# The last expert's down product: column halves of w_down one after the other, with scatter, squares and products between them

## The reference

```python
def expert_choice_swiglu(h, w_router, w_gate, w_up, w_down):
    cap = EC_CAPACITY_FACTOR * seq // N_EXPERTS          # 64
    aff = softmax(h @ w_router)
    g, idx = top_k(swapaxes(aff, 1, 2), cap)             # each expert its 64 tokens
    xin = h[idx]
    a, u = xin @ w_gate, xin @ w_up                      # 64 x 1024 x 1024 each, per expert
    y = (silu(a) * u) @ w_down * g[..., None]
    return zeros.at[idx].add(y)                          # scattered back to the tokens
...
x = x + expert_choice_swiglu(rms_norm(x, norm2_g), ...)
return rms_norm(x, normf_g)
```

## Time and profile before

| | us |
|---|---|
| median of 3 runs | 883.68 (882.5 to 883.97) |
| span of the profiled execution (first to last instruction) | 882.2 |
| the profiled execution's own time around the span | not given apart |
| TensorE busy in the span | 853.8 (97%) |
| VectorE, ScalarE, GpSimd busy | 358.2, 268.3, 26.9 |
| last matmul of the last down ends | 869.41 |
| first output transfer issued | 874.81 |

### The profile page before, as it was taken

The page is one execution under the profiler, slowest core; times in us unless marked ns, Lnnn a source line. Parts: engine busy times, 40 slices in busy tenths (PEclk is TensorE's granted clock), DMA queues, the critical chain, the costliest instruction groups (busy, mean ns, idle before and its releaser), DMA issues.

```text
span 882.2 us, 10559 instructions
## 1 busy us (share of the span) xinstructions
PE 853.8 (97%) x4287; PEld 522.3 (59%) x4287; DVE 358.2 (41%) x638; ACT 268.3 (30%) x469; POOL 26.9 (3%) x47
## 2 busy tenths in 40 slices
PE   9999999999999999999999999999998988988996
PEld 8898876687878888889534443343433433334332
DVE  5378877576606344327322313132221311311413
ACT  6233766685624233227101010010100101001213
POOL 1050000000000000002000000000000000000001
PEclk9999999999999999999999999999999999999999
DMA  9730212023134335843999999999999999999993
GB/s 287 166 96 1 72 48 96 1 68 89 42 120 115 107 86 145 316 204 144 387 408 417 422 429 429 428 428 428 426 427 426 428 427 427 428 429 429 427 418 152
DMA packets 80372, 238.70 MB, mean 271 GB/s; under 512 B 8003, under 2 KB 63427, under 8 KB 65605
## 3 DMA queue, kind: packets, MB, share of 16 engines
q1 hardware_dynamic: 75040, 235.94, 67.9%
q10 hardware_dynamic: 5284, 2.09, 1.0%
HBM read 235.92 MB, written 2.10 MB: 270 GB/s over the span
## 4 chain that ended last, share of the span: by engine, by line
PE 81%; DMA 11%; DVE 3%; ACT 2%; issue 1%; ACTq 0%; POOL 0%; DVEq 0%; POOLq 0%; SPq 0%
PE psum L1521 18%; PE psum L1553 12%; DMA wslot<-in_w_down 11%; PE psum L1054 11%; PE psum L1055 10%; PE psum L1056 10%; PE psum L1478 3%; PE psum L1572 3%; PE psum L1236 2%; PE psum L1248 2%; PE psum L1206 1%; PE psum L1222 1%; PE psum L1533 1%; PE psum L1486 1%; PE psum L1258 1%
## 5 line engine op out<-in xcount | busy, mean ns | idle before, releaser
L1521 PE MATMUL psum<-wslot,xinT 128*64 128x512 f32 x1016 | 226.9, 595 | 5.8 <-DMA wslot<-in_w_gate 2.7
L1521 PEld LDWEIGHTS psum<-wslot,xinT 128*64 128x64 f32 x1016 | 70.3, 137 | 145.6 <-issue 133.9
L1553 PE MATMUL psum<-wslot,actT 128*64 128x512 f32 x504 | 114.1, 597 | 8.7 <-DMA wslot<-in_w_down 8.7
L1054 PE MATMUL psum<-hT_hi,w_hi 128*128 128x512 f32 x208 | 82.8, 398 | 0.0
L1056 PE MATMUL psum<-hT_hi,w_lo 128*128 128x512 f32 x208 | 81.2, 391 | 0.0
L1055 PE MATMUL psum<-hT_lo,w_hi 128*128 128x512 f32 x208 | 81.2, 391 | 0.0
L1553 PEld LDWEIGHTS psum<-wslot,actT 128*64 128x64 f32 x504 | 34.7, 137 | 76.4 <-issue 69.0
L1748 DVE TENSOR_TENSOR w_lo<-w_raw,w_hi 128x1024 fp32r<-128x1024 f32 (+1 forms) x46 | 52.9, 1174 | 52.7 <-ACT w_hi L706 52.6
L993 ACT ACTIVATE actT<-psum 128x512 f32<-128x512 f32 x16 | 9.6, 598 | 185.5 <-PE psum L1533 185.5
L2123 DVE TENSOR_TENSOR x<-x,psum 128x512 f32<-128x512 f32 x56 | 34.7, 682 | 74.7 <-PE psum L1572 74.7
L2115 DVE TENSOR_TENSOR y_lo<-psum,y_hi 64x512 fp32r<-64x512 f32 x32 | 22.0, 689 | 103.1 <-ACT y_hi L1003 102.6
(11 more groups left out here) (268 smaller groups left out, 1303.9 us busy)
## 6 DMA issues: line engine op xcount, KB each, us to landing
wslot<-in_w_gate SPq DMA_DIRECT2D x27, 2048.0 KB, 29.3
wslot<-in_w_up SPq DMA_DIRECT2D x27, 2048.0 KB, 29.9
wslot<-in_w_down SPq DMA_DIRECT2D x24, 2048.0 KB, 28.3
w_raw<-in_w_in SPq DMA_DIRECT2D x34, 512.0 KB, 4.8
wslot<-in_w_down SPq DMA_DIRECT2D x15, 1024.0 KB, 30.5
wslot<-in_w_gate SPq DMA_DIRECT2D x10, 1024.0 KB, 11.3
wslot<-in_w_up SPq DMA_DIRECT2D x9, 1024.0 KB, 10.7
w_raw<-in_w_out SPq DMA_DIRECT2D x8, 512.0 KB, 5.0
```

The costliest lines, as they stand in the source:

```text
L1054: pe.matmul(out_, s_hi, m_hi, start=(k == 0), stop=False)
L1521: mm = pe.matmul(bank[2 * e + n][CAP * f:CAP * f + CAP, :], xinT[:, HALF * h + k, CAP * e:CAP * e + CAP], wslot[place_of(m)][:, k % PART, ...
L1553: mm = pe.matmul(bank[4 + e][CAP * f:CAP * f + CAP, :], actT[:, e, k, CAP * h:CAP * h + CAP], wslot[place_of(m)][:, k % PART, SEQ * f:SEQ ...
```

## The change

The last expert's down runs per column half. Its w_down is loaded in four quarters, each four steps k (one h) by 512 columns, in the order (h, f) = (0,0), (1,0), (0,1), (1,1), into the same four places. `last_down(h, f)` issues the four matmuls of a quarter. y of f = 0 is taken out, scattered, and for tiles 0 and 1 squared and multiplied by the gain, between the quarters; add_rows(2,0) moves in front of the second quarter. Pieces are now scattered and squared with f = 0 first. `GAINED` holds the four pieces of f = 0: VectorE multiplies them by the gain early, and they are scaled later, (3,0) and (2,0) by ScalarE, (0,0) and (1,0) by VectorE in SBUF. Where both ScalarE and VectorE read a piece from PSUM, one waits for the other. GpSimd's three counters become one, and the squares' scrap buffer moves.

```diff
-        LAST_PIECES = [(0, 0), (1, 0), (0, 1), (1, 1), (3, 0), (3, 1), (2, 0), (2, 1)]
-        SQUARED = [(c, f) for c in SUM_TILES for f in range(2)]
-        GAINED = [(1, 1), (3, 0)]
-        FINISHED = [(0, 0), (0, 1), (1, 0), (3, 1), (2, 0), (2, 1)]
-        OUT_PIECES = [(0, 0), (0, 1), (1, 0), (1, 1), (3, 1), (3, 0), (2, 0), (2, 1)]
+        LAST_PIECES = [(c, f) for f in range(2) for c in SUM_TILES]
+        SQUARED = LAST_PIECES
+        GAINED = [(1, 0), (0, 0), (2, 0), (3, 0)]
+        GAINED_FIRST = [(1, 0), (2, 0)]
+        SCALED_ACT = [(3, 0), (2, 0)]
+        FINISHED = [(0, 1), (0, 0), (1, 1), (1, 0), (3, 1), (2, 1)]
+        OUT_PIECES = [(0, 1), (0, 0), (1, 1), (1, 0), (3, 0), (3, 1), (2, 0), (2, 1)]
...
+                if m >= LAST_DOWN:
+                    f, h = divmod(m - LAST_DOWN, 2)
+                    rows = rows_of((LAST_DOWN + 2 * h) // 2).rearrange("p (k n) -> p k n", k=HALF)
+                    sp.dma_start(by_columns(m), rows[:, :, SEQ * f:SEQ * f + SEQ]).then_inc(w_slot_in[place], 16)
+                    return
...
                 for f in range(2):
+                    if last:
+                        wait_part_used(act_, last_part(1, f))
                     act_.activation(y_hi[CAP * e:CAP * e + CAP, SEQ * f:SEQ * f + SEQ],
                                     bank[4 + e][CAP * f:CAP * f + CAP, :], ACT.Copy).then_inc(y_hi_done, 1)
+                    if last and f == 0:
+                        square_sum(0)
+                        square_sum(1)
...
+            def last_down(h, f, between):
+                p, m = PAIRS - 1, last_part(h, f)
+                wait_part_in(pe, m)
+                for k in range(HALF):
+                    mm = pe.matmul(bank[5][CAP * f:CAP * f + CAP, :], actT[:, 1, k, CAP * h:CAP * h + CAP],
+                                   by_columns(m)[:, k, :], start=(h == 0 and k == 0), stop=(h == 1 and k == HALF - 1))
+                    if k == HALF - 1:
+                        mm.then_inc(w_slot_used[place_of(m)], 1)
+                    between(k)
...
+            def behind_first(k):
+                if k == 1:
+                    add_rows(1, 0)
+                if k == 3:
+                    pe.wait_ge(y_lo_done, 4 * (PAIRS - 1) + 2)
+                    add_rows(2, 0)
...
+            last_down(0, 0, behind_first)
+            last_down(1, 0, behind_others)
+            last_down(0, 1, behind_others)
             pe.wait_ge(y_hi_done, 4 * PAIRS - 1)
+            pe.wait_ge(y_lo_done, 4 * PAIRS - 1)
+            give_rows(0, 0)
+            give_rows(1, 0)
+            last_down(1, 1, behind_others)
+            give_rows(3, 0)
+            give_rows(2, 0)
             pe.wait_ge(y_hi_done, 4 * PAIRS)
             pe.wait_ge(y_lo_done, 4 * PAIRS)
+            give_rows(0, 1)
+            give_rows(1, 1)
+            give_rows(3, 1)
             add_rows(2, 1)
+            give_rows(2, 1)
...
+                    if (p, e, f) == (PAIRS - 1, 1, 0):
+                        dve.wait_ge(gf_done, 2)
+                        gain(1, 0)
+                        gain(0, 0)
...
             def finish(c, f):
                 cols = slice(SEQ * f, SEQ * f + SEQ)
                 dve.wait_ge(rstd3, SUM_TILES.index(c) + 1)
+                if (c, f) in GAINED:
+                    dve.wait_ge(gained, GAINED.index((c, f)) + 1)
+                    dve.tensor_scalar(fin[:, c, cols], fin[:, c, cols], rstd[:, c:c + 1], None, ALU.mult)\
+                        .then_inc(fin_done, 1)
+                    return
...
-            gain(1, 1)
+            gain(2, 0)
             gain(3, 0)
```

More of the change, by code:

```diff
@@ L202, in encoder_block @@
     fin = sb("fin", [NT, D], W0)
-    junk = sb("junk", [2, SEQ], 60)
+    junk = sb("junk", [2, SEQ], 105.5)
     g2 = small[:, 8:16]
@@ L245, in encoder_block @@
         sumsq_done = sem("sumsq_done")
-        ms_done = sem("ms_done")
+        pool_step = sem("pool_step")
         rstd_done = sem("rstd_done")
@@ L257, in encoder_block @@
         a_sumsq = sem("a_sumsq")
-        a_ms = sem("a_ms")
         a_rstd = sem("a_rstd")
@@ L287, in encoder_block @@
         sumsq2 = sem("sumsq2")
-        ssq2_summed = sem("ssq2_summed")
         rstd2 = sem("rstd2")
@@ L335, in encoder_block @@
         ssq3 = sem("ssq3")
-        ssq3_summed = sem("ssq3_summed")
         rstd3 = sem("rstd3")
@@ L428, in encoder_block, with last_part, by_columns @@
         tenants = [[m for m in range(N_PARTS) if place_of(m) == i] for i in range(SLOTS + len(ONCE))]
+        LAST_DOWN = N_PARTS - 4
+        def last_part(h, f):
+            return LAST_DOWN + 2 * f + h
+        def by_columns(m):
+            return wslot[place_of(m)].rearrange("p k n -> p (k n)").rearrange("p (k n) -> p k n", k=HALF)
         def turn_of(m):
@@ L613, in _ @@
                 cols = slice(SEQ * f, SEQ * f + SEQ)
-                if (c, f) in GAINED:
-                    sp.wait_ge(fin_act_done, GAINED.index((c, f)) + 1)
+                if (c, f) in SCALED_ACT:
+                    sp.wait_ge(fin_act_done, SCALED_ACT.index((c, f)) + 1)
                 else:
@@ L626, in _, with settle, power, power_of_means @@
             pool.wait_ge(neg_half_set, 1)
-            def power(sums, into, n, width, counted, done, first):
-                pool.tensor_scalar(into, sums, 1.0 / width, EPS, ALU.mult, ALU.add).then_inc(counted, 1)
-                pool.wait_ge(counted, first + 1)
+            steps = [0]
+            def settle(ins):
+                ins.then_inc(pool_step, 1)
+                steps[0] += 1
+                pool.wait_ge(pool_step, steps[0])
+            def power(sums, into, n, width, done):
+                settle(pool.tensor_scalar(into, sums, 1.0 / width, EPS, ALU.mult, ALU.add))
                 pool.tensor_tensor(into, into, neg_half[:, 0:n], ALU.pow).then_inc(done, 1)
-            def power_of_means(c, i):
+            def power_of_means(c):
                 first, second = (ssq_half[:, 2 * c + f:2 * c + f + 1] for f in range(2))
-                pool.wait_ge(ssq3, 2 * i + 2)
-                pool.tensor_scalar(rstd[:, c:c + 1], second, first, EPS, ALU.add, ALU.add).then_inc(ssq3_summed, 1)
-                pool.wait_ge(ssq3_summed, i + 1)
+                pool.wait_ge(ssq3, SQUARED.index((c, 1)) + 1)
+                settle(pool.tensor_scalar(rstd[:, c:c + 1], second, first, EPS, ALU.add, ALU.add))
                 pool.tensor_tensor(rstd[:, c:c + 1], rstd[:, c:c + 1], neg_half[:, 0:1], ALU.pow).then_inc(rstd3, 1)
@@ L643, in rstd_of_x @@
                 pool.wait_ge(sumsq_done, c + 1)
-                power(ssq[:, c:c + 1], rstd[:, c:c + 1], 1, D, ms_done, rstd_done, c)
+                power(ssq[:, c:c + 1], rstd[:, c:c + 1], 1, D, rstd_done)
             for c in range(NT):
@@ L651, in _ @@
                 pool.wait_ge(a_sumsq, c + 1)
-                power(ssqA[:, w * c:w * c + w], rstdA[:, w * c:w * c + w], w, HD, a_ms, a_rstd, c)
+                power(ssqA[:, w * c:w * c + w], rstdA[:, w * c:w * c + w], w, HD, a_rstd)
             for c in range(NT):
@@ L657, in _ @@
                     pool.wait_ge(sumsq2, NT + 1)
[L658 to L661, removed]
+                    settle(pool.tensor_tensor(ssq[:, c:c + 1], ssq[:, c:c + 1], ssq_half[:, 0:1], ALU.add))
+                power(ssq[:, c:c + 1], rstd[:, c:c + 1], 1, D, rstd2)
             pool.wait_ge(logits_done, NT)
@@ L673, in _ @@
             pool.memset(ones_row[0:1, :], 1.0).then_inc(ones_row_set, 1)
-            for i, c in enumerate(SUM_TILES):
-                power_of_means(c, i)
+            for c in SUM_TILES:
+                power_of_means(c)
         @block.scalar
@@ L997, in high_y @@
             def high_y(p, e):
-                wait_part_used(act_, part_at(p, w_down, 1, e, HALF - 1))
+                last = (p, e) == (PAIRS - 1, 1)
+                if not last:
+                    wait_part_used(act_, part_at(p, w_down, 1, e, HALF - 1))
                 if p and e == 0:
@@ L1002, in high_y, with square_sum @@
                 for f in range(2):
+                    if last:
+                        wait_part_used(act_, last_part(1, f))
                     act_.activation(y_hi[CAP * e:CAP * e + CAP, SEQ * f:SEQ * f + SEQ],
                                     bank[4 + e][CAP * f:CAP * f + CAP, :], ACT.Copy).then_inc(y_hi_done, 1)
+                    if last and f == 0:
+                        square_sum(0)
+                        square_sum(1)
+            def square_sum(n):
+                c, f = SQUARED[n]
+                wait_sum(act_, c, f)
+                if (c, f) in GAINED_FIRST:
+                    act_.wait_ge(gained, GAINED.index((c, f)) + 1)
+                if n >= 2:
+                    act_.wait_ge(ssq3, n - 1)
+                act_.activation(junk[:, n % 2, :], sum_of(c, f), ACT.Square, scale=D ** -0.5,
+                                accum_out=ssq_half[:, 2 * c + f:2 * c + f + 1]).then_inc(ssq3, 1)
             read_first_xin(0)
@@ L1031, in _ @@
```

(59 more changed lines are left out.)

## The result

The changed kernel takes 890.68 us (median of 4 runs, 889.9 to 891.29), the kernel before 883.45 (4 runs). The ratio is 1.0077 (95% interval 1.0064 to 1.0090), that is +6.8 us (+5.7 to +8.0). The forecast was 891.6, with a range of 888.5 to 894.5 and a chance of 0.93 for slower. The profiled execution has a span of 889.3, 7.1 us more than before, and a time of 891.07, 1.8 around the span.

The account below looks back on a forecast made before the run. TensorE's matmuls were taken to bound the end until 869.41, then the tail until 882.2. Terms +6.2 + 0.66 + 1.1 + 0 - 0.1 = +7.9 on 883.68 gave 891.6 us, range 888.5 to 894.5.

Parts of the forecast that it names:

- last down, alone: Last expert's down on TensorE: 32 records take 13.3 us instead of 7.1, +6.2 us (bounds 0 and +7.9).
- tail from T1: Behind the last down matmul: first output issued 5.35 us later, end +12.7 against +12.8, so -0.1 us (bounds -0.95, +0.8).
- No transfer was waited for: Before the last down's final steps: the last weight part lies ready about 1.7 us early, so no wait can be removed.
- A lone record costs 0.43 us: Last down on TensorE: a record without a neighbour in the other array half takes 0.43 us, against 0.221 now.
- Rival A: Last down: a record costs 0.221 us alone as well, time 885.3 us (884.5 if the end follows the last piece); chance 0.06.
- rival B: ScalarE behind the last down: halves cost nothing and squares bound the tail; span 0.8 us less, time perhaps 881.4; chance 0.03.
- Rival D: Last down: part of the overlap stays, pace about 0.33 us, +3.5 us instead of +6.2, time 889 us; chance 0.06.
- One record overlaps at the change of half: Last down, where f = 0 ends and f = 1 begins: one record overlaps, taking 13.8 us to 13.3.
- The estimate from the Trainium skill: Last down: 1.59 times for two column tiles, lone half 11.3 us instead of 13.3, sum +5.9 us instead of +7.9.
- Loads cost nothing: Four quarter loads in 2 KB runs: slower, but the first has 3 us of slack; cost 0 (bounds 0 and +1 us).
- rival C: TensorE's granted clock falls while half the array works: some 901 us; chance 0.06 together with anything else above 894.
- rival E: Last down: the first half runs early, but the second half is already there, not on its way; part of the forecast.

Follow-up runs that it names:

- groups of four and two: The kernel before with the last expert's down matmuls issued in groups of four, or of two, steps k per column half: ratios 1.0037 and 0.9999.

## Why the prediction was right

In the table T0 and T1 are the ends of the last down before and after.

| step | forecast | measured |
|---|---|---|
| last down, alone | +6.2 (13.3 against 7.1) | +5.4 (12.51 against 7.09) |
| add_rows(2,0) inside | +0.66 | +0.66 |
| four scatters inside | +1.1 | +1.12 |
| start of the last down | 0 | +0.13 |
| T1 - T0 | +8.0 | +7.33 |
| tail from T1 | -0.1 | -0.23 |
| span | +7.9 | +7.1 |

- *No transfer was waited for.* Right: the earlier trace rows showed it, and leaving out the last load changes nothing (1.0002). What the change wanted to hide wasn't there. The slack was smaller than the prediction read from the bytes, though: the last part was issued at 835.4 and landed 31.2 us later, at 866.6, so it lay ready 0.9 us before 867.5 and not 1.7.
- *A lone record costs 0.43 us.* Right: 1.71 us for 4 and 3.59 for 8, and the order alone, in the kernel before, costs 5.1 us in its chain. Rival A (0.221) would have left 7.1, rival B needed that too. Rival D's "part of the overlap stays" is true in a way it didn't say: not a middling pace, but full overlap for four records at each change of half.
- *One record overlaps at the change of half.* This term was mis-sized: four do, three more than forecast (-1.3 us), while starting again behind `add_rows` and the scatters costs 0.15 us three times (+0.45), which the forecast had left out. Together the term is 0.8 us too high, as is the sum. The groups of four and two show the overlap in two more places.
- The estimate from the Trainium skill (TensorE: Matmul & The Clock Gate, "Part 3: Packing small matmuls"), 11.3 us for the lone half and +5.9 for the sum, was 1.2 us too low, mine 0.8 too high. The estimated factor for two tiles isn't borne out: a lone record's pace is 1.71/4 = 0.43 against 0.221 in pairs, 1.9 times and not 1.59; the 12.51 us come from full loss in most places and none at the change of half.
- *Loads cost nothing.* Right for this kernel, and only for it: at 391 GB/s they are slower. The first quarter landed at 859.7 (issued at 828.1, 31.6 us to landing) and was needed at 861.6, so it had 1.9 us of slack and not 3. The kernel with pairs and quarter loads stood still 1.5 us ahead of the last down.
- *Tail.* Right in place and size (5.28 for 5.3, 12.56 for 12.7): the square of (2,0) held the first output, and moving it gave 0.5 us back. The reading of the kernel before was wrong in one point: its end hung on the fourth piece, not on the first. That didn't touch the sum, which took the 12.8 from the trace.
- *The clock* (rival C): 1.00 until TensorE stopped, through a last down with 12.5 us of mostly lone halves. This rival is out.
- *The first half early, the second on its way* (rival E): the first half did run early, and the second was there 5.5 us before its last quarter was begun, as forecast.

## What to carry to other kernels

Where two matmuls fill half of the array each and run side by side, neither may be left without the other. Issuing all of one half first costs 1.7 times the time here (12.21 us against 7.09), and changing over every four records nothing (7.12). The danger is visible beforehand, from the spacing of weight loads against that of a whole-width matmul. Before hiding a transfer, look when it lands and when it is needed; TensorE had been busy without a gap since 800 us here, so a later transfer was not what it waited for. And what runs early is worth only what the end then gains: here the first output still hung on the second half.

## What was not expected

- At a change of half, TensorE takes up four records of the new half beside the last four of the old one: groups of four records a half cost 7.12 us for 32 records (pairs: 7.09), groups of eight 10.55, sixteen 12.21.
- Issued in pairs, the records of both halves start and end together; a semaphore on the first of the last pair brought y_hi no earlier.
- An output of 64 partitions moves at 187 GB/s with the DMA engines 0.82 busy, where one of 128 moves at 379 with 1.02: leaving out half the partitions saved no time.
- The first output need not be the one that sets the end: where the fourth comes late, the DMA engines run dry before it, and the end hangs on that one.
- Loads in 2 KB runs go at 383 to 389 GB/s against 418 to 434 in 8 KB runs (windows of 1 us from 857 to 861).
